# Placing the softmax and scan steps by weight, and remainders of the first branch in turns

## The chip, the core and the metric

The kernel runs on one core of a Trainium2 chip. The metric is the time of one execution in device microseconds. Three executions of the kernel before took 1069.21, 1072.25 and 1073.41 us; their median is 1072.25. Five engines work beside each other: PE (TensorE, with its weight loads shown as PEld), DVE (VectorE), ACT (ScalarE), POOL (GpSimd) and SP (SyncE, which issues transfers). Each runs its own list of instructions in the order in which they were written; what one needs from another it waits for on a semaphore.

## The reference, cut to what matters

Three network blocks follow one another on 256 tokens of width 1024 in float32. The change lies in the first one:

```python
h = rms_norm(x, norm1_g)
(dq, dk, dv, iq, ik, iw, nq, nkv, ng, sz, sxbc, sdt, mg) = split(h @ w_in)
y_a = dsa_mixer(...)                       # softmax attention over keys chosen by top-k
y_b = nsa_mixer(...)                       # compressed, selected and window attention
y_c = ssd_mixer(sz, sxbc, sdt, ...)        # short convolution, chunked scan, gate by silu(sz), norm
gates = sigmoid(mg)                        # three gates of width 1024
mix = gates[0] * (y_a @ w_br_dsa) + gates[1] * (y_b @ w_br_nsa) + gates[2] * (y_c @ w_br_ssd)
x = x + mix @ w_out
x = x + square(relu(rms_norm(x, norm2_g) @ w_ff1)) @ w_ff2
```

The second block and the final norm are left as they are by the change.

## The kernel before

Every product with a weight matrix is a job: one tile of 128 output columns by 256 tokens, accumulated in a PSUM bank of p_proj over eight blocks of 128. There are three such banks. The products are made in two parts each: a weight tile w is split into w_hi, a copy rounded to the matrix format (ACT, L1052, into ring_hi with 3 slots), and the remainder w - w_hi (L658, into ring_lo), and the activations are split in the same way (L1082 for the copy, L666 for the low part). A job is then 24 matmuls, w_hi by hi, w_hi by lo and w_lo by hi (L2056 to L2058). Weights stream into a ring of 5 slots and are used in the order of the jobs.

The planner writes one list of steps; each engine takes from it its own share, in that order. The middle of the first block is the loop over `wide`, a list of 80 jobs, numbered here 0 to 79:

- 0 to 3 gates (mg); 4 to 39 twelve times two convolution inputs (xbc) and a gate; 40 to 55 the scan's gate (sz); 56 to 63 the last eight mg; 64 to 71 br_dsa (the first branch's product); 72 to 79 br_nsa.

Behind each job stands a share of `filler`, 89 groups of other work, spread evenly by count:

- `soft`, 53 groups, one softmax step of an attention head each, as a pipeline: scores (sA, PE L1904 into p_score, released by DVE), exponentials (sE, ACT), probabilities (sR), transposes (sB, PE L1914 into the one bank p_turn, read by ACT), values (sC, PE L1932 into p_pv). Some groups carry a compressed-attention step too (pA L1883, pB, pT: four transposes L1891 into p_turn, copied out by ACT at L979) or a top-k selection on DVE (up to L1505), which a later sA waits for (`select_done`).
- `prep`, 15 groups: transposes of the convolved inputs (btr L1949; xtr L1943 into p_turn, read by DVE at L1598), states (st L1963), and others.
- `quads`, 21 groups, the scan for one of 16 head groups each: uE (ACT L1037 and L1045), the decay products on POOL (L795, L799), uB (PE L1976 into p_pv, then DVE L1619 and L1624). From step 8 on a group also holds the split of two finished tiles (ACT L1082), their squares (ACT L1118), the sum of squares over channels (PE L1988 into p_mean) and the scaled low parts (DVE L1363). The last group is the norm of the scan's output (ynorm).

So a group that holds two rows in the list stands behind one job when the count is ahead: in the kernel before, jobs 7, 14, 21, 28, 35, 42, 56, 63 and 70 carry two groups and all others one. Softmax steps end at job 46, transposes stand in jobs 47 to 57, scan steps (uE) start at job 61.

Other work stands at fixed places behind the group: the convolution of a job (xconv, DVE L1578 to L1583, which reads the bank of p_proj) behind the next job, the products with the gates (DVE L1725 for sz, L1742 for br_dsa, L1745 and L1747 for br_nsa; POOL L807 for a part of the mg gates), and the splits of the branches: the first four tiles of br_dsa's input ahead of job 63's group, the other four behind it. br_dsa's low parts alternate between DVE (even) and POOL (odd).

Who makes a remainder is set by `on_gpsimd(u)`: always POOL for some names, br_dsa among them, otherwise in turns by the number of the tile:

```python
def on_gpsimd(u):
    if unit_of[u] in ("br_dsa", "dq", "nq", "val_glu", "b_gate", "a_gate", "xr"):
        return True
    ...
    return hi_turn[u] % 2 == 0
```

The copy and the remainder of a tile that is used four jobs later stand behind each job (the steps `wsplit`).

## Time and profile before

| | |
|---|---|
| three executions | 1069.21, 1072.25, 1073.41 us |
| median | 1072.25 us |
| profiled execution | 1073.69 us |
| span of the profile | 1072.0 us |
| mean granted clock of TensorE | 0.987 |
| PE busy | 1019.9 us (95%) |
| DVE busy | 673.4 us (63%) |
| ACT busy | 618.6 us (58%) |
| POOL busy | 589.4 us (55%) |

The span is what the profiler saw from the first to the last instruction; the profiled execution's own time is 1.7 us longer. PE is busy for nearly all of it. Of the 1072 us the loop over `wide` takes the stretch from 122 to about 490 us. The granted clock is a share of full speed, 2.4 GHz; 0.5 is the lower level, 1.2 GHz.

### The profile page before, as it was taken

The numbers are of one execution on the slowest core, as the hardware profiler recorded it, in microseconds if no ns is written. First come the engines' busy times: TensorE is split into PE (matmuls) and PEld (weight loads), VectorE is DVE, ScalarE is ACT, GpSimd is POOL, SyncE is SP. The second block draws the span as 40 slices with busy tenths as digits, with TensorE's granted clock in tenths as the row PEclk, the third lists the DMA queues.
The fourth block names the chain that finished last, engine by engine and source line by source line (L and its number), as shares of the span: only waits on it lengthen the run. The fifth ranks groups of instructions, "written<-read, shape, count | busy, mean of one in ns | idle before, by whom it ended". The sixth has DMA issues, their size and how long they took to land. (4 is left out here: it accounts for less than half of the span.)

```text
span 1072.0 us, 19547 instructions
## 1 busy us (share of the span) xinstructions
PE 1019.9 (95%) x7235; PEld 922.5 (86%) x7235; DVE 673.4 (63%) x1441; ACT 618.6 (58%) x1246; POOL 589.4 (55%) x448
## 2 busy tenths in 40 slices
PE   8999999999999998889999999999899989899996
PEld 8799878888889997789989999878898977689985
DVE  7769687666564426685545554232699986478873
ACT  5455566766665448764446555344434548568853
POOL 3657344444545449844543434444768876467563
PEclk9999999999999998999999999999999999999998
DMA  8334333343333455435655555655555545634452
GB/s 311 99 119 138 119 118 99 101 120 116 100 102 116 153 177 169 153 97 178 216 180 174 180 185 187 197 176 177 158 158 158 182 152 157 216 119 146 140 171 95
DMA packets 45822, 163.76 MB, mean 153 GB/s; under 512 B 5216, under 2 KB 5280, under 8 KB 45216
## 3 DMA queue, kind: packets, MB, share of 16 engines
q1 hardware_dynamic: 43200, 158.25, 47.0%
q10 hardware_dynamic: 2528, 4.26, 1.4%
q8 instruction: 58, 0.95, 0.4%
q14 instruction: 36, 0.29, 0.1%
HBM read 161.41 MB, written 1.08 MB: 152 GB/s over the span
## 5 line engine op out<-in xcount | busy, mean ns | idle before, releaser
L658 POOL TENSOR_TENSOR ring_lo<-ring,ring_hi 128x1024 fp32r<-128x1024 f32 x176 | 425.1, 2419 | 280.3 <-ACT ring_hi L1052 279.5
L2056 PE MATMUL p_proj<-arena_r,ring_hi 128*128 128x256 f32 x1664 | 499.2, 300 | 11.0 <-POOL ring_lo L658 5.0
L2057 PE MATMUL p_proj<-arena_r,ring_hi 128*128 128x256 f32 x1664 | 473.9, 285 | 0.0
L2058 PE MATMUL p_proj<-arena_r,ring_lo 128*128 128x256 f32 x1664 | 473.8, 285 | 0.0
L1052 ACT ACTIVATE ring_hi<-ring 128x1024 fp32r<-128x1024 f32 x276 | 289.5, 1054 | 118.7 <-PE p_proj L1814 63.5
L2056 PEld LDWEIGHTS p_proj<-arena_r,ring_hi 128*128 128x128 f32 x1664 | 322.0, 194 | 27.8 <-issue 15.8
L2057 PEld LDWEIGHTS p_proj<-arena_r,ring_hi 128*128 128x128 f32 x1664 | 322.4, 194 | 7.2 <-issue 6.0
L2058 PEld LDWEIGHTS p_proj<-arena_r,ring_lo 128*128 128x128 f32 x1664 | 322.1, 194 | 0.0
L658 DVE TENSOR_TENSOR ring_lo<-ring,ring_hi 128x1024 fp32r<-128x1024 f32 x100 | 130.8, 1308 | 113.8 <-ACT ring_hi L1052 112.5
L1812 PE MATMUL p_proj<-ring_hi,arena_r 128*128 128x512 f32 x272 | 107.8, 396 | 8.0 <-POOL ring_lo L658 5.3
L1814 PE MATMUL p_proj<-ring_lo,arena_r 128*128 128x512 f32 x272 | 106.1, 390 | 0.0
L1813 PE MATMUL p_proj<-ring_hi,arena_r 128*128 128x512 f32 x272 | 106.0, 390 | 0.0
L773 POOL TENSOR_TENSOR sbuf_s<-sbuf_s,srow 128x256 f32<-128x256 f32 (+1 forms) x48 | 41.8, 871 | 83.3 <-DVE srow L1565 58.7
L1812 PEld LDWEIGHTS p_proj<-ring_hi,arena_r 128*128 128x128 f32 x272 | 51.1, 188 | 22.0 <-POOL ring_lo L658 7.8
L1082 ACT ACTIVATE arena_r<-arena 128x256 fp32r<-128x256 f32 x108 | 42.7, 409 | 39.5 <-DVE arena L1747 22.5
L1814 PEld LDWEIGHTS p_proj<-ring_lo,arena_r 128*128 128x128 f32 x272 | 51.1, 188 | 10.9
L1813 PEld LDWEIGHTS p_proj<-ring_hi,arena_r 128*128 128x128 f32 x272 | 51.1, 188 | 10.0
L666 POOL TENSOR_TENSOR arena_r<-arena,arena_r 128x256 fp32r<-128x256 f32 x59 | 45.5, 783 | 25.4 <-ACT arena_r L1082 25.4
L1214 ACT ACTIVATE th<-p_proj 128x256 f32<-128x256 f32 x44 | 16.9, 384 | 57.8 <-PE p_proj L2058 57.7
L1553 DVE CUSTOM_DVE_ANT_0 sbuf_s<-p_score,caus,nrq 128x128 f32<-128x128 f32 (+1 forms) x64 | 24.2, 415 | 41.0 <-PE p_score L1904 40.8
L1658 DVE SCALAR_TENSOR_TENSOR p_score<-arena,par,p_score 128x256 f32<-128x256 f32 x116 | 47.0, 483 | 1.2
L987 ACT ACTIVATE sbuf_s<-sbuf_s,srow 128x128 f32<-128x128 f32 (+1 forms) x96 | 42.6, 449 | 3.1 <-DVE srow L1553 3.1
(345 smaller groups left out, 1277.7 us busy)
## 6 DMA issues: line engine op xcount, KB each, us to landing
ring<-w_stream SPq DMA_DIRECT2D x286, 512.0 KB, 3.5
arena<-run_d ACTq DMA_DIRECT2D x11, 256.0 KB, 3.9
arena<-w_tok SPq DMA_DIRECT2D x1, 1632.0 KB, 12.6
arena<-w_rgi SPq DMA_DIRECT2D x1, 1536.0 KB, 6.1
wide_a<-run_d ACTq DMA_DIRECT2D x5, 256.0 KB, 4.0
arena<-x_t SPq DMA_DIRECT2D x4, 256.0 KB, 6.6
arena<-w_cmp SPq DMA_DIRECT2D x1, 1024.0 KB, 15.8
sbuf_s<-x_tok SPq DMA_DIRECT2D x1, 1024.0 KB, 5.6
```

Source lines behind the costliest of these rows:

```text
L658: return eng.tensor_tensor(ring_lo[:, u % RING, :, :].rearrange("p k n -> p (k n)"), ring[:, u % RING, :, :].rearrange("p k n -> p (k n)") ...
L666: return eng.tensor_tensor(lo(c), src(c), hi(c).bitcast(F32), ALU.subtract)
L987: ins = act.activation(p, p, ACT.Exp, bias=srow[:, i % 4, 2 + h:3 + h], scale=-1.0, accum_out=srow[:, i % 4, 4 + h:5 + h])
L1052: act.activation(ring_hi[:, hi_slot[u], :, :].rearrange("p k n -> p (k n)"), ring[:, u % RING, :, :].rearrange("p k n -> p (k n)"), ACT.Copy)\
L1082: ins = act.activation(hi(c), src(c), ACT.Copy)
L1658: ins = dve.scalar_tensor_tensor(out=A(AC + cc) if tap == CONV_K - 1 else acc, in0=ub[:, cc, tap:tap + S], scalar=col("even_cw", CONV_K * ...
L1812: pe.matmul(slot(key), hi, w_hi, start=(c == 0), stop=False)
L1813: pe.matmul(slot(key), lo, w_hi, start=False, stop=False)
L1814: mm = pe.matmul(slot(key), hi, w_lo, start=False, stop=(c == n - 1))
L2056: pe.matmul(slot(s)[:, 0:S], w_hi, hi, start=(c == 0), stop=False)
L2057: pe.matmul(slot(s)[:, 0:S], w_hi, lo, start=False, stop=False)
L2058: mm = pe.matmul(slot(s)[:, 0:S], w_lo, hi, start=False, stop=(c == n - 1))
```

## The change

The groups are no longer spread by count, but by weight. Each group has a number of units: 12 for the first ten softmax steps, 10 for the other 43, 8 for each group of `prep` and 15 for each scan group, 985 in all. A group is placed behind job n if its accumulated end does not go beyond (n + 1) / 78 of 985, that is 12.63 units per job. The order of the groups among themselves stays. And br_dsa leaves the list of `on_gpsimd`, so that its eight remainders take turns by their number: four stay on POOL and four go to DVE.

```diff
--- before.py
+++ after.py
@@ -1,3 +1,4 @@
+import itertools
 from contextlib import ExitStack
 
 import concourse.bass as bass
@@ -220,6 +221,7 @@
         quads.append(group)
     quads.append([("ynorm",)])
     filler = soft + prep + quads
+    ends = list(itertools.accumulate([12] * 10 + [10] * 43 + [8] * len(prep) + [15] * len(quads)))
     mg = jobs["mg"]
     wide = []
     wide += mg[0:4]
@@ -235,8 +237,7 @@
             out += [("split", "dsa", c) for c in range(4)]
         if job[1] == "br_dsa":
             out.append(("split", "nsa", job[2]))
-        want = (n + 1) * len(filler) // (len(wide) - 2)
-        while at < min(want, len(filler)):
+        while at < len(filler) and ends[at] * (len(wide) - 2) <= (n + 1) * ends[-1]:
             out += filler[at]
             at += 1
         if job == mg[23]:
@@ -637,7 +638,7 @@
         unit_half = {u: s[2] for u, s in enumerate(opening(steps)) if s[0] == "tm"}
 
         def on_gpsimd(u):
-            if unit_of[u] in ("br_dsa", "dq", "nq", "val_glu", "b_gate", "a_gate", "xr"):
+            if unit_of[u] in ("dq", "nq", "val_glu", "b_gate", "a_gate", "xr"):
                 return True
             if unit_of[u] == "even_yb" and unit_half[u] == 0:
                 return True
```

Lines of the changed kernel are numbered one higher than those of before from here on (L1904 is L1905, L658 is L659).

The placement that follows: two softmax steps stand in jobs 11, 15, 19, 22, 26, 30, 34, 38 and 41, and one in each other job up to 43; job 7 now has one. Transposes and states stand in jobs 44 to 51, with two groups in 44 (btr and the first xtr), 46, 47 and 49 (a state and a transpose) and 51 (the last two xtr). Scan steps start at job 55, one per job, with none in jobs 59, 65 and 71, and job 63 has one. ynorm stays in job 77.

PE, behind job 7, before. The names: sbuf_s are probabilities, sbuf_t their transposes, tok the values, kk_d keys, and arena_r the split activations.

```order
L1914 MATMUL p_turn<-ident,sbuf_s 128x128 [waits p_ready,turn_read_act]
L1914 MATMUL p_turn<-ident,sbuf_s 128x128
L1932 MATMUL p_pv<-sbuf_t,tok 64x128 [waits turn_read_act,pv_read_act]
L1932 MATMUL p_pv<-sbuf_t,tok 64x128
L1904 MATMUL p_score<-kk_d,arena 128x2x128 [waits score_read_dve]
L1914 MATMUL p_turn<-ident,sbuf_s 128x128 [waits p_ready,turn_read_act]
L1914 MATMUL p_turn<-ident,sbuf_s 128x128
L1932 MATMUL p_pv<-sbuf_t,tok 64x128 [waits turn_read_act,pv_read_act]
L1932 MATMUL p_pv<-sbuf_t,tok 64x128
L1904 MATMUL p_score<-kk_d,arena 128x512 [waits select_done,score_read_dve]
L2056 MATMUL p_proj<-arena_r_51,ring_hi 128x256 [waits w_lo_dve,proj_read_dve,proj_read_act]
```

And in the changed kernel:

```order
L1915 MATMUL p_turn<-ident,sbuf_s 128x128 [waits p_ready,turn_read_act]
L1915 MATMUL p_turn<-ident,sbuf_s 128x128
L1933 MATMUL p_pv<-sbuf_t,tok 64x128 [waits turn_read_act,pv_read_act]
L1933 MATMUL p_pv<-sbuf_t,tok 64x128
L1905 MATMUL p_score<-kk_d,arena 128x2x128 [waits score_read_dve]
L2057 MATMUL p_proj<-arena_r_51,ring_hi 128x256 [waits w_lo_dve,proj_read_dve,proj_read_act]
```

The second step, whose scores wait for the selection (`select_done`), now stands behind job 8, and job 8's first matmul directly behind the first step.

POOL, from the gate of job 62 to the second job of br_dsa, before. sqb and root are tiles that hold gates, arena_r_55 and arena_r_56 are the low parts of br_dsa's input, and sbuf_s with kk_s is a scan product.

```order
L807 TENSOR_SCALAR sqb<-sqb 128x256 [waits proj_read_act]
L799 TENSOR_TENSOR sbuf_s<-sbuf_s,kk_s 128x512 [waits l_ready]
L658 TENSOR_TENSOR ring_lo<-ring,ring_hi 128x1024 [waits w_hi_ready]
L807 TENSOR_SCALAR root<-root 128x256 [waits proj_read_act]
L666 TENSOR_TENSOR arena_r_55<-arena,arena_r_51 128x256 [waits hi_dsa] x2
L799 TENSOR_TENSOR sbuf_s<-sbuf_s,kk_s 128x512 [waits l_ready] x2
L666 TENSOR_TENSOR arena_r_56<-arena,arena_r_52 128x256 [waits hi_dsa] x2
L658 TENSOR_TENSOR ring_lo<-ring,ring_hi 128x1024 [waits w_hi_ready]
L799 TENSOR_TENSOR sbuf_s<-sbuf_s,kk_s 128x512 [waits l_ready]
L658 TENSOR_TENSOR ring_lo<-ring,ring_hi 128x1024 [waits w_hi_ready]
```

The same place in the changed kernel:

```order
L808 TENSOR_SCALAR sqb<-sqb 128x256 [waits proj_read_act]
L800 TENSOR_TENSOR sbuf_s<-sbuf_s,kk_s 128x512 [waits l_ready]
L659 TENSOR_TENSOR ring_lo<-ring,ring_hi 128x1024 [waits w_hi_ready]
L808 TENSOR_SCALAR root<-root 128x256 [waits proj_read_act]
L667 TENSOR_TENSOR arena_r_55<-arena,arena_r_51 128x256 [waits hi_dsa] x2
L800 TENSOR_TENSOR sbuf_s<-sbuf_s,kk_s 128x512 [waits l_ready]
L667 TENSOR_TENSOR arena_r_56<-arena,arena_r_52 128x256 [waits hi_dsa] x2
L796 TENSOR_TENSOR sbuf_t<-sbuf_t,arena 128x512 [waits l_ready]
L800 TENSOR_TENSOR sbuf_s<-sbuf_s,kk_s 128x512 [waits pool_chain]
L659 TENSOR_TENSOR ring_lo<-ring,ring_hi 128x1024 [waits w_hi_ready]
```

The remainder between the two gates has stayed. Between the two pairs of low parts stands one scan product in place of two. Behind the second pair stood a remainder and one scan product; now the two products of a step of the scan's second half (L796, L800) come first and a remainder behind them.

DVE, before, from the product with the gate of the first br_dsa job (job 64) on. L1742 is the product with the gate, L666 a low part of the next branch, L1619 and L1624 read the scan products.

```order
L1742 TENSOR_TENSOR arena<-p_proj,arena 128x256 [waits mg_ready,proj_filled,lo_dsa]
L666 TENSOR_TENSOR arena_r_57<-arena,arena_r_53 128x256 [waits hi_nsa,proj_read_dve]
L1619 SCALAR_TENSOR_TENSOR p_pv<-arena,par,p_pv 128x128 [waits pv_done,lo_nsa]
L1619 SCALAR_TENSOR_TENSOR p_pv<-arena,par,p_pv 128x128
L1624 TENSOR_TENSOR arena<-p_pv,arena 128x128 [waits dve_chain]
L1624 TENSOR_TENSOR arena<-p_pv,arena 128x128
L1742 TENSOR_TENSOR arena<-p_proj,arena 128x256 [waits mg_ready,proj_filled,pv_read_dve]
L666 TENSOR_TENSOR arena_r_57<-arena,arena_r_53 128x256 [waits hi_nsa,proj_read_dve]
L1619 SCALAR_TENSOR_TENSOR p_pv<-arena,par,p_pv 128x128 [waits pv_done,lo_nsa]
L1619 SCALAR_TENSOR_TENSOR p_pv<-arena,par,p_pv 128x128
L1624 TENSOR_TENSOR arena<-p_pv,arena 128x128 [waits dve_chain]
L1624 TENSOR_TENSOR arena<-p_pv,arena 128x128
```

The same engine in the changed kernel, from the remainder ahead of that product on:

```order
L659 TENSOR_TENSOR ring_lo<-ring,ring_hi 128x1024 [waits w_hi_ready,lo_dsa]
L1743 TENSOR_TENSOR arena<-p_proj,arena 128x256 [waits mg_ready,proj_filled,w_lo_dve]
L667 TENSOR_TENSOR arena_r_57<-arena,arena_r_53 128x256 [waits hi_nsa,proj_read_dve]
L1620 SCALAR_TENSOR_TENSOR p_pv<-arena,par,p_pv 128x128 [waits pv_done,lo_nsa]
L1620 SCALAR_TENSOR_TENSOR p_pv<-arena,par,p_pv 128x128
L1625 TENSOR_TENSOR arena<-p_pv,arena 128x128 [waits dve_chain]
L1625 TENSOR_TENSOR arena<-p_pv,arena 128x128
L1743 TENSOR_TENSOR arena<-p_proj,arena 128x256 [waits mg_ready,proj_filled,pv_read_dve]
L667 TENSOR_TENSOR arena_r_57<-arena,arena_r_53 128x256 [waits hi_nsa,proj_read_dve]
L659 TENSOR_TENSOR ring_lo<-ring,ring_hi 128x1024 [waits w_hi_ready,lo_nsa]
L1743 TENSOR_TENSOR arena<-p_proj,arena 128x256 [waits mg_ready,proj_filled,w_lo_dve]
L667 TENSOR_TENSOR arena_r_57<-arena,arena_r_53 128x256 [waits hi_nsa,proj_read_dve]
```

Two of the four remainders that DVE has taken over (L659) stand here, each ahead of a product with the gate, and the step of the scan between the second and the third of these products is gone, since job 65 has none.

## Rows read from the trace of the kernel before

**Rows 1.** The page's busy times: us, share of the span, instructions.

```profile
PE 1019.9 (95%) x7235; PEld 922.5 (86%) x7235; DVE 673.4 (63%) x1441; ACT 618.6 (58%) x1246; POOL 589.4 (55%) x448
```

**Rows 2.** Timeline, PE: start, us, engine, line, output and inputs, pieces, idle before.

```profile
395.24 0.28 PE L2056 MATMUL p_proj<-arena_r,ring_hi 128*128 128x256 f32 x1
...
398.12 0.28 PE L2056 MATMUL p_proj<-arena_r,ring_hi 128*128 128x256 f32 x1
```

**Rows 3.** Timeline, PE, the steps behind job 7 and the start of job 8.

```profile
150.94 0.70 PE L1904 MATMUL p_score<-kk_d,arena 128*128 128x256 f32 x2
...
153.11 1.10 PE L1904 MATMUL p_score<-kk_d,arena 128*128 128x512 f32 x2 [0.89 <-DVE arena L1505]
154.67 0.35 PE L2056 MATMUL p_proj<-arena_r,ring_hi 128*128 128x256 f32 x1 [0.46 <-issue]
```

**Rows 4.** Timeline, DVE, the convolution of job 5.

```profile
153.06 1.51 DVE L1583 SCALAR_TENSOR_TENSOR arena<-p_proj,half,arena 128x253 f32<-128x253 f32 x3
```

**Rows 5.** Timelines, PE, ACT and DVE: users of the bank p_turn.

```profile
191.99 0.60 PE L1891 MATMUL p_turn<-ident,arena 128*128 128x128 f32 x4
...
192.74 0.59 ACT L979 ACTIVATE arena<-p_turn 128x512 f32<-128x512 f32 x1
...
352.14 0.69 DVE L1598 TENSOR_TENSOR arena<-p_turn,sp 128x512 f32<-128x512 f32 x1
...
381.04 0.66 PE L1943 MATMUL p_turn<-ident,arena 128*128 128x128 f32 x4 [0.85 <-DVE arena L1598]
```

**Rows 6.** Timeline, PE, scan products behind jobs 63 and 64.

```profile
403.97 0.66 PE L1976 MATMUL p_pv<-sbuf_s,arena 128*64 128x128 f32 x8
...
409.88 1.12 PE L1976 MATMUL p_pv<-sbuf_s,arena 128*64 128x128 f32 x8 [5.26 <-DVE arena L1624]
...
416.35 0.66 PE L1976 MATMUL p_pv<-sbuf_s,arena 128*64 128x128 f32 x8
```

**Rows 7.** Timelines, POOL (three rows) and DVE, around job 64.

```profile
405.84 2.54 POOL L658 TENSOR_TENSOR ring_lo<-ring,ring_hi 128x1024 fp32r<-128x1024 f32 x1
...
408.89 1.41 POOL L666 TENSOR_TENSOR arena_r<-arena,arena_r 128x256 fp32r<-128x256 f32 x2
410.26 2.51 POOL L799 TENSOR_TENSOR sbuf_s<-sbuf_s,kk_s 128x512 f32<-128x512 f32 x2
...
405.41 3.25 DVE L666 TENSOR_TENSOR arena_r<-arena,arena_r 128x256 fp32r<-128x256 f32 x2 [10.39 <-ACT arena_r L1082]
```

**Rows 8.** Windows: stretch, us, busy PE, PEld, DVE, ACT, POOL, PEclk, DMA share, GB/s.

```profile
409.70:416.50 6.80, 6.62 (x34) 6.07 (x36) 2.84 (x7) 4.47 (x12) 6.80 (x6) 0.52 0.29 82
443.90:447.30 3.40, 3.40 (x14) 3.03 (x14) 1.95 (x6) 3.37 (x10) 0.84 (x1) 0.54 0.09 32
```

**Rows 9.** Waits of PE between 122 and 490 us: total, times, longest.

```profile
PE p_pv L1976 <- DVE arena L1624: 10.6, 5, 5.3
```

**Rows 10.** Timeline, PE, the scan's second half.

```profile
442.53 0.45 PE L1976 MATMUL p_pv<-sbuf_s,arena 128*64 128x128 f32 x4 [2.70 <-DVE arena L1624]
...
449.11 0.45 PE L1976 MATMUL p_pv<-sbuf_s,arena 128*64 128x128 f32 x4
...
454.11 0.45 PE L1976 MATMUL p_pv<-sbuf_s,arena 128*64 128x128 f32 x4
...
483.30 1.43 PE L1988 MATMUL p_mean<-th,mean_d 128*128 128x256 f32 x4 [1.65 <-ACT th L1118]
```

**Rows 11.** Timeline, DVE, two turns of the scan's second half.

```profile
469.56 0.49 DVE L1624 TENSOR_TENSOR arena<-p_pv,arena 128x128 f32<-128x128 f32 x2
...
472.66 2.65 DVE L1747 TENSOR_TENSOR arena<-arena,sqb 128x256 f32<-128x256 f32 x1
...
475.99 0.49 DVE L1624 TENSOR_TENSOR arena<-p_pv,arena 128x128 f32<-128x128 f32 x2
...
479.08 1.22 DVE L658 TENSOR_TENSOR ring_lo<-ring,ring_hi 128x1024 fp32r<-128x1024 f32 x1 [1.56 <-ACT ring_hi L1052]
...
481.91 0.49 DVE L1624 TENSOR_TENSOR arena<-p_pv,arena 128x128 f32<-128x128 f32 x2
```

## The prediction

> **What bounds the kernel now.** I read the page's busy times first: PE is busy for 1019.9 us of the span of 1072.0, so the time is PE's work plus the stretches in which PE waits or runs at half clock [rows 1]. The change adds and removes no instruction, so only those stretches can move. I number the wide jobs as the list `wide` does: jobs 0 to 39 alternate gate and convolution products, 40 to 55 are sz, 56 to 63 the last gates, 64 to 71 br_dsa and 72 to 79 br_nsa. A job with no step behind it takes 2.88 us [rows 2]. Between 122 and 490 us, where the moved steps stand, the list of waits gives PE three kinds of lost time.
>
> First, job 7 carries two softmax steps. PE waits 0.89 us for the end of a top-k selection on DVE and then 0.46 us before job 8, whose bank is free only when DVE ends the convolution of job 5 (row 153.06: ends at 154.57, PE starts at 154.67) [rows 3, 4]. That is 1.35 us. A pair of transposes at job 56 costs another 0.85 us [rows 5].
>
> Second, jobs 63 and 64. Two scan steps stand in job 63, beside the eight splits of the first branch. From the end of job 63 (403.97) to the end of job 64 (416.35) pass 12.4 us [rows 6]. The work in it is two groups of scan products at about 0.66 us and one job, 4.2 us with the gaps. So 8.2 us are lost: 5.26 idle, and job 64 at a clock of 0.52 [rows 6, 8]. Behind it stands POOL, which has a remainder of 2.54 us, two low parts (1.41 us), two scan products (2.51 us) and again two low parts in a row [rows 7].
>
> Third, the second half of the scan (steps 8 to 15, in jobs 70 to 78). Of PE's waits on L1624 (10.6 us in five) 5.3 us remain beside the 5.26, and 1.65 us on L1118 come to them [rows 9, 10]. After two of these waits the granted clock is 0.54 for 3.4 us, worth 1.6 us each [rows 8]. Together 10.2 us. In all the stretch loses 1.35 + 0.85 + 8.2 + 10.2 = 20.6 us.
>
> **The change part by part: the first ten steps (jobs 0 to 10).** They get 12 units against an even 12.6 per job, so job 7 keeps one softmax step and its second one goes to job 8. PE then reaches job 8 early, at 151.6 (the end of the product that began at 150.94). Nothing on DVE ahead of the convolution that frees the bank has moved, so job 8 starts at 154.67 as before. PE idles 3.0 us instead of 1.35: a loss of 1.7. The step itself is only done later. After idles of 2.70 and 1.65 us the clock was at 0.54 for 3.4 us [rows 8, 10]. I therefore charge another 1.6 us, bounds 0 and 1.6.
>
> **The other softmax steps (jobs 11 to 43).** Pairs now stand in jobs 11, 15, 19, 22, 26, 30, 34, 38 and 41 instead of every seventh job. A pair costs nothing beyond its work where the bank p_turn is read in time. In job 15 it is not: the transposes of the compressed probabilities (L1891) now stand directly ahead of the next step's transposes in the one bank, and ACT's copy of them ends at 193.33 where PE is done with them near 192.4. PE waits about 1.0 us where job 15 hid it before [rows 5]. For the other eight pairs I take 0; the bound is 0.5 each, 4 us, if ACT falls behind.
>
> **Transposes and states (jobs 44 to 51).** Two steps in a job share p_turn twice: btr with the first transpose in job 44, and the last two in job 51. The pair of job 56 cost 0.85 [rows 5]; I take 0.85 for job 44. In job 51 an sz gate stands on DVE ahead of the reading transposed tile (row 352.14 took 0.69 us), so the second waits about 1.4. Together 2.25 against 0.85: a loss of 1.4.
>
> **The scan's first half and the remainders in turns (jobs 55 to 64).** Steps now start at job 55, one per job, where ACT has room. Four of the eight remainders of br_dsa go to DVE, at 1.22 us (row 479.08) instead of some 2.4. Job 63 has one scan step. I count from the end of its products, T. POOL does a remainder until T+2.6, the last gate until 3.0, two low parts until 4.4, one scan product until 5.7, two low parts until 7.1 [rows 7]. DVE's even low parts stand behind the same POOL instructions: the pair at 405.41 took 3.25 us and ended just after the remainder of 405.84 [rows 7]. The last piece of job 64 starts at T+7.1 and the job ends near T+7.5; its work needs 3.5. So 4.0 us are idle, and I add 1.0 for the clock (bounds 0 and 2.4): 5.0 instead of 8.2, a gain of 3.2.
>
> **The scan's second half (jobs 66 to 77).** This is the largest term. Without waits PE takes 5.0 us for a job with such a step (449.11 to 454.11) [rows 10]. But a ring of DVE and ACT turns once per step: DVE reads the products and ends L1624; ACT then splits and squares two tiles and after that splits the next weights; DVE waits for these, makes the remainder, reads the job's bank, and only then reads the next products. From 476.48 to 482.40 one turn takes 5.9 us with the remainder on DVE; from 470.05 to 476.48 it takes 6.4 with the remainder on POOL, since L1747 took 2.65 us beside it [rows 11]. The turns in br_dsa hold a low part (L666) in place of L1747, so I keep about 6.0. Seven turns from step 8 to step 15 take 42 us. Before, the jobs 71 to 76 lay beside them; now 68 to 75, two more, because jobs 65 and 71 carry no step. PE's own work beside the seven turns is 8 × 2.88 + 7 × 1.9 = 36 us, so 6 us remain idle, in pieces of 0.2 to 1.6. One fall of the clock, half of it inside such waits, adds 0.8. That is 6.8 instead of 10.2, a gain of 3.4; bounds 2 (the turns shrink to PE's pace) and 12.
>
> The Trainium skill (page "SBUF — State Buffer", section "SBUF: two separate sides") says that GpSimd and a DVE instruction with two SBUF inputs share a port pair as an exclusive lock: the one that starts second is blocked until the other has ended. The trace agrees: L1747 began at 472.66 and ended at 475.31, while POOL's remainder ran [rows 11]. By that rule alone a remainder moved to DVE may stand behind a whole POOL instruction, which speaks against the turns; what it would give is the second rival.
>
> **The sum.** After: 4.6 + 1.0 + 2.25 + 5.0 + 6.8 = 19.6 us lost, 1.0 less than the 20.6. The profiled execution took 1073.69 (span 1072.0 and 1.7 around it); 1.0 less is 1072.7. That run lies 1.4 above the median of the three, 1072.25, so on the scale of the median I say **1071.2 us**. A measurement of this kernel can tell about 0.5% (5.4 us) from no change.
>
> **The rivals.** *The late stretch runs at PE's pace* (chance 0.29). POOL loses 4 × 2.4 = 9.6 us of work around jobs 62 to 69, and DVE's blocked instructions shrink with it. For it: POOL is what stands in the way in rows 7, and two jobs without steps break the ring. Against it: the ring has 5.9 us even where POOL is idle [rows 11]. The second half then loses 2 us instead of 6.8, and jobs 63 and 64 lose 2.7 (no fall of the clock, and DVE's low parts are early) instead of 5.0: 7.1 us off, 1064.1.
>
> *DVE becomes the bound* (chance 0.11, the slower side). Each of the four remainders put on DVE stands in the ring. If each waits for a whole POOL instruction (1.3 to 2.4 us), the four turns in br_dsa take 8 us instead of 6. It decides from about 1.3 us per remainder on, because that is the slack that jobs 65 and 71 give. Four times 1.8 us is 7.2; one more fall of the clock is 1.6: 8.8 us more, 1080.0.
>
> *The first idle does not come* (chance 0.10). If DVE reaches the bank of job 8 earlier, or PE makes the time up, the 3.3 us of the first part vanish: 1067.9. Against it stands the unchanged order on DVE.
>
> *The steps move and nothing follows* (chance 0.05): every wait is only put elsewhere, 1072.2.
>
> **How the numbers follow.** My forecast has the remaining 0.45; its own range is 1066 to 1076, from the clock charge of job 8 (1.6 less), the eight pairs (up to 4 more) and the second half (3 either way). The range reaches into the first rival and ends short of the second: 1063 to 1077.5. Faster by over 0.5% (below 1066.9): nearly all of the first rival, a third of the third and a tenth of the forecast, 0.35. Slower (above 1077.6): nearly all of the second and little of the forecast, 0.12. Within 0.5%: 0.53.
>
> **What would show it.** In the trace of the changed kernel PE should idle about 3 us ahead of job 8, with a clock near 0.5 behind it; about 1 us behind the second L1891 group; 0.9 and 1.4 us in the paired transposes near 350 to 375 us; some 4 us, in pieces, in the first job of br_dsa. The ring should turn every 6 us, with PE waits of 0.2 to 1.6 us on L1624's successor. I am wrong if PE waits under 2 us in all from job 65 to 78, if the clock stays at full ahead of job 9, or if the softmax pairs show waits on p_turn.

## The result: 1077.3 us against 1072.5

The changed kernel took 1077.34 us, the median of 20 executions (1072.15 to 1080.46); the kernel before, measured beside it, took 1072.53 us (20 executions). The ratio, which goes by all executions and not by the two medians, is 1.0032, with a 95% interval of 1.002 to 1.0044. The forecast was 1071.2 us, a little faster. The change made the kernel a little slower: by 4.8 us in the medians and 3.4 us by the ratio. That is inside the 0.5% that the prediction called no change, but the interval lies clear of no change, on the other side of it than the forecast. 1077.34 us lies outside the forecast's own range (1066 to 1076) and just inside the wide one (1063 to 1077.5).

The page of the changed kernel begins with the busy times of the engines. They answer to [rows 1]; the span is 1076.0 us, 4.0 more than before, in an execution of 1077.98 us.

```profile
PE 1024.1 (95%) x7235; PEld 925.3 (86%) x7235; DVE 683.8 (64%) x1445; ACT 619.1 (58%) x1246; POOL 583.1 (54%) x444
```

The four remainders that moved are to be seen here (DVE 4 instructions more, POOL 4 fewer). PE makes the same 7235 matmuls and is busy 4.2 us longer: a matmul at half clock counts as busy. Where PE waits, its list of waits between 122 and 490 us tells (total us, times, longest). It answers to [rows 9].

```profile
PE p_proj L2057 <- issue: 5.5, 3, 3.0
PE p_proj L2057 <- DVE arena_r L667: 3.5, 1, 3.5
PE p_pv L1977 <- DVE arena L1625: 2.0, 2, 1.3
PE p_turn L1944 <- DVE arena L1599: 1.3, 1, 1.3
PE p_proj L2057 <- POOL arena_r L667: 1.2, 2, 0.7
PE p_turn L1915 <- ACT arena L980: 0.8, 1, 0.8
PE p_turn L1944 <- ACT kk_d L1013: 0.7, 1, 0.7
PE p_turn L1915 <- ACT sbuf_t L997: 0.3, 1, 0.3
```

The 10.6 us on the scan's sums (L1624 before) have become 2.0. In their place stand jobs that wait for low parts (L667) or start late ("issue": 3.0 ahead of job 8, 2.1 ahead of job 64), and four waits on the bank p_turn. PE's timeline at the four places, as in [rows 3, 5, 6]:

```profile
150.78 0.70 PE L1905 MATMUL p_score<-kk_d,arena 128*128 128x256 f32 x2
154.51 0.35 PE L2057 MATMUL p_proj<-arena_r,ring_hi 128*128 128x256 f32 x1 [3.03 <-issue]
...
199.22 0.66 PE L1915 MATMUL p_turn<-ident,sbuf_s 128*128 128x128 f32 x4 [0.78 <-ACT arena L980]
...
413.53 0.66 PE L1977 MATMUL p_pv<-sbuf_s,arena 128*64 128x128 f32 x8
416.28 0.36 PE L2057 MATMUL p_proj<-arena_r,ring_hi 128*128 128x256 f32 x1 [2.09 <-issue]
417.35 0.39 PE L2057 MATMUL p_proj<-arena_r,ring_hi 128*128 128x256 f32 x1 [0.48 <-POOL arena_r L667]
420.41 0.58 PE L2057 MATMUL p_proj<-arena_r,ring_hi 128*128 128x256 f32 x1 [0.72 <-POOL arena_r L667]
...
463.04 0.58 PE L2057 MATMUL p_proj<-arena_r,ring_hi 128*128 128x256 f32 x1 [3.51 <-DVE arena_r L667]
```

The clock is in the windows (columns as in [rows 8]; the granted clock is the third number from the end):

```profile
155.30:158.70 3.40, 3.40 (x18) 3.40 (x17) 0.83 (x4) 1.03 (x2) 2.88 (x2) 0.50 0.02 5
418.20:428.40 10.20, 9.46 (x45) 8.31 (x44) 6.15 (x9) 5.25 (x12) 8.88 (x6) 0.50 0.29 93
463.40:469.30 5.90, 5.90 (x30) 4.99 (x30) 4.67 (x9) 3.23 (x7) 1.81 (x2) 0.50 0.27 89
```

PE was at the lower level, 1.2 GHz, for 3.4 us behind the wait ahead of job 8, for 10.2 us from inside job 64 on, and for 5.9 us behind the wait inside job 72. If half of PE's busy time there is counted as lost, that is 1.7, 4.7 and 2.95 us.

Half is a little too much. A third profile of the same kernel (E14 below) has the same wait ahead of job 8 and no half clock behind it. These are its rows of job 8's start and of the wait in job 15:

```profile
154.92 0.36 PE L2057 MATMUL p_proj<-arena_r,ring_hi 128*128 128x256 f32 x1 [3.02 <-issue]
...
198.14 0.66 PE L1915 MATMUL p_turn<-ident,sbuf_s 128*128 128x128 f32 x4 [0.78 <-ACT arena L980]
```

From the one to the other pass 43.22 us, against 44.71 us (154.51 to 199.22) in the first profile. So 3.4 us at half clock cost 1.5 us, 44% of the busy time, and by that price the three stretches cost 1.5, 4.2 and 2.6 us.

From these rows the sum of the prediction can be made again, with what was measured (the clock at half of the busy time, as the prediction counts it):

| stretch | lost before | forecast | idle, measured | clock, measured | lost, measured |
|---|---|---|---|---|---|
| jobs 7 and 8 | 1.35 | 4.6 | 3.03 | 1.7 | 4.7 |
| job 15 | 0 | 1.0 | 0.78 | 0 | 0.8 |
| the bank p_turn, jobs 41 to 56 | 0.85 | 2.25 | 0.33 + 0.69 + 1.29 | 0 | 2.3 |
| jobs 63 to 65 | 8.2 | 5.0 | 2.09 + 0.48 + 0.72 | 4.7 | 8.0 |
| the scan's second half | 10.2 | 6.8 | 0.72 + 1.32 + 3.51 | 2.95 | 8.5 |
| sum | 20.6 | 19.6 | 15.0 | 9.4 | 24.3 |

24.3 against 20.6 is 3.7 of the 4.0 us between the two spans; with 44% in place of half it is 23.3 against 20.4, and 2.9 of the 4.0 us. Every forecast of a loss is there. Of the two forecasts of a gain, that of jobs 63 to 65 is not there (8.0 against 8.2 us before) and that of the scan's second half came by half (8.5 against 10.2, where 6.8 was forecast).

### The profile page after: what moved, and what is told of

It reads as the page before. It is cut to its first block and busy times, and to the rows that moved or that the text cites. A ratio compares the mean times of both kernels' runs of the same rounds, so it can differ in the third digit from the quotient of the medians.

```text
span 1076.0 us, 19551 instructions
## 1 busy us (share of the span) xinstructions
PE 1024.1 (95%) x7235; PEld 925.3 (86%) x7235; DVE 683.8 (64%) x1445; ACT 619.1 (58%) x1246; POOL 583.1 (54%) x444
## 5 line engine op out<-in xcount | busy, mean ns | idle before, releaser
L659 POOL TENSOR_TENSOR ring_lo<-ring,ring_hi 128x1024 fp32r<-128x1024 f32 x172 | 415.4, 2419 | 286.4 <-ACT ring_hi L1053 285.6
L659 DVE TENSOR_TENSOR ring_lo<-ring,ring_hi 128x1024 fp32r<-128x1024 f32 x104 | 138.4, 1331 | 115.9 <-ACT ring_hi L1053 114.6
L667 POOL TENSOR_TENSOR arena_r<-arena,arena_r 128x256 fp32r<-128x256 f32 x59 | 46.4, 798 | 25.6 <-ACT arena_r L1083 25.5
```

What stands on the lines that cost most here:

```text
L659: return eng.tensor_tensor(ring_lo[:, u % RING, :, :].rearrange("p k n -> p (k n)"), ring[:, u % RING, :, :].rearrange("p k n -> p (k n)") ...
L667: return eng.tensor_tensor(lo(c), src(c), hi(c).bitcast(F32), ALU.subtract)
```

## The experiments

All of them were timed beside the kernel before. Its medians in the four groups below were 1073.0, 1071.9, 1072.1 and 1072.0 us, so kernels of different groups are compared by their ratios to it.

### One part of the change at a time

E1 has the new placement alone, with br_dsa's remainders all on POOL:

```diff
-            if unit_of[u] in ("dq", "nq", "val_glu", "b_gate", "a_gate", "xr"):
+            if unit_of[u] in ("br_dsa", "dq", "nq", "val_glu", "b_gate", "a_gate", "xr"):
```

> The changed kernel with br_dsa back among the remainders that POOL always makes, so only the new placement is left. The changed kernel took 1077.3 us, the one before 1072.5. Theory (the placement costs, the turns in themselves give a little): around jobs 63 to 65 POOL has two remainders of 2.4 us more, so PE's waits there, 3.3 us in the changed kernel, grow by about 2 us, and the time is 1078 to 1081. Rival (the remainders on DVE stand in the ring of the scan's second half and make job 72 late): without them the wait of 3.5 us ahead of job 72 goes and the time falls to 1073 to 1075.

E2 is the kernel before with the turns alone, the same line changed the other way.

> The kernel before with only br_dsa taken from the list, so the steps stand as before and four of eight remainders go to DVE. Theory (the placement costs, the turns give): the wait of 5.26 us behind job 63 shrinks by one remainder of POOL, about 2.4 us, and the time is 1069 to 1071. Rival (the turns cost): DVE's remainders stand in the ring of the scan's second half, PE's waits on the sums that DVE writes grow, and the time is 1074 to 1077.

E3 is the changed kernel with the first thirteen steps back where they stood:

```diff
-[12] * 10 + [10] * 43 + [8] * len(prep)
+[12] * 8 + [5, 12, 12, 12, 13] + [10] * 40 + [8] * len(prep)
```

> The changed kernel with the first thirteen softmax steps placed as in the kernel before (two behind job 7, one each behind jobs 8 to 12); the rest of the placement is that of the changed kernel. Theory: the idle time of 3.0 us ahead of job 8 becomes 1.35 us as before and the half clock behind it (about 1.5 us lost) does not come, so the time is 1073.5 to 1075. Rival (what PE wins there it loses again in the next waits, because another engine sets the pace): within 1 us of the changed kernel, 1076.5 to 1078.

E4 moves one scan step from job 72 to job 71:

```diff
-[15] * len(quads)
+[15] * 15 + [14, 16] + [15] * 4
```

> The changed kernel with one weight lowered by one unit and the next raised by one, so that the scan step of job 72 stands behind job 71 and job 72 has none. Theory (job 72 is the first to use the last low part of br_nsa's input, which DVE makes late behind POOL's remainder, and a job 71 without a step brings PE there too early): the wait of 3.5 us ahead of the last block of job 72 goes, the half clock behind it too (about 2.9 us lost), a wait of 1 to 2 us on DVE's sums comes in job 71, and the time is 1072 to 1075. Rival (the ring of DVE and ACT is simply 6 us behind PE, wherever PE meets it): the idle time moves to the next step's wait in full, and the time is 1076 to 1078.

| kernel | median us | ratio to before | interval |
|---|---|---|---|
| changed | 1077.34 | 1.0032 | 1.002 to 1.0044 |
| E1, placement alone | 1077.80 | 1.0046 | 1.0023 to 1.0068 |
| E2, turns alone | 1070.43 | 0.9979 | 0.9968 to 0.999 |
| E3, first steps as before | 1073.03 | 1.0003 | 0.999 to 1.0016 |
| E4, step in job 71 | 1078.19 | 1.0054 | 1.0035 to 1.0073 |

The wide spacing of the first ten steps costs 3 to 4 us (E3 against the changed kernel), as the theory had it, though the time is half a microsecond below its range: in E3's profile PE waits 0.89 and 0.46 us there as before, and the first stretch at half clock is gone. The rest of the placement with the turns is worth nothing (E3 against before: 1.0003).

The turns alone are worth 2 to 3 us on the old placement, and nothing on the new one (E1 against the changed kernel, whose intervals lie over each other). Neither expectation of E1 had that. Its waits show an exchange: ahead of job 64 and inside it 2.7 and 0.4 us in place of 2.1, 0.5 and 0.7; on the scan's sums 0.6 in place of 2.0; inside job 72 4.8 in place of 3.5. E2's time lies where its theory had it, but not for the reason given: the wait behind job 63 fell only from 5.3 to 4.7 us, not by 2.4. From that wait's end to the scan products behind job 64 E2 takes 5.1 us, the kernel before 6.5, of which 6.4 lie at half clock.

In E4 the rival held. Two rows of its waits, PE between 122 and 490 us:

```profile
PE p_pv L1977 <- DVE arena L1625: 5.3, 5, 1.7
...
PE p_proj L2057 <- DVE arena_r L667: 0.5, 1, 0.5
```

The wait of 3.5 us inside job 72 is nearly gone, and the waits on the scan's sums have grown from 2.0 to 5.3 us. It was not job 72 that was badly placed: the turn of DVE and ACT lags behind PE, and PE meets the lag at whatever comes first.

### The bank p_turn, the turns exchanged, and other places for the scan

For E5 the weights are replaced by a list with a job for each group, as for all that follow. It has E3's first steps, then softmax pairs behind jobs 14, 18, 21, 24, 28, 31, 35 and 38, a state and a transpose together in jobs 47 to 50 and all other transposes alone; the scan stands as in the changed kernel:

```diff
+    where = [0, 1, 2, 3, 4, 5, 6, 7, 7, 8, 9, 10, 11, 12, 13, 14, 14, 15, 16, 17, 18, 18, 19, 20, 21, 21, 22, 23,
+             24, 24, 25, 26, 27, 28, 28, 29, 30, 31, 31, 32, 33, 34, 35, 35, 36, 37, 38, 38, 39, 40, 41, 42, 43,
+             44, 45, 46, 47, 47, 48, 48, 49, 49, 50, 50, 51, 52, 53, 54,
+             54, 55, 56, 57, 58, 60, 61, 62, 63, 64, 66, 67, 68, 69, 70, 72, 73, 74, 75, 76, 77]
-        while at < len(filler) and ends[at] * (len(wide) - 2) <= (n + 1) * ends[-1]:
+        while at < len(filler) and where[at] <= n:
```

> The kernel with the first steps as before (1073.0 us), and in it the pairs moved so that no two users of the bank p_turn stand directly behind each other: softmax pairs behind jobs 7, 14, 18, 21, 24, 28, 31, 35 and 38, and the transposes one per job from 44 on, a state and a transpose together in four jobs; scan steps as in the changed kernel. Theory (the four waits on p_turn, 0.78 + 0.32 + 0.69 + 1.28 us, are a plain loss): 3.1 us less, 1069.5 to 1070.5. Rival (PE gets earlier to the scan, which POOL, DVE and ACT pace, and waits longer there): 1072 to 1073.5.

E6 is E3 with the turns of br_dsa exchanged: POOL and DVE each make the other's four remainders.

```diff
         def on_gpsimd(u):
+            if unit_of[u] == "br_dsa":
+                return hi_turn[u] % 2 > 0
```

> The kernel with the first steps as before (1073.0 us), and in it the turns of br_dsa's remainders exchanged: the four of DVE on POOL and the four of POOL on DVE. Theory (the remainder that POOL makes as job 63 ends holds up DVE's first low parts, and through them job 64): PE's wait of 2.1 us ahead of job 64 falls to about 1 us, the two waits behind it go, the fall of the clock there with them, and the time is 1069 to 1071. Rival (the other remainders come to stand in the way in their turn, POOL's next one ahead of its own low parts): 1072 to 1075.

E7 is E3 with the scan steps of jobs 63 and 64 one job later, so that job 63 has none.

> The kernel with the first steps as before (1073.0 us), and in it the scan steps of jobs 63 and 64 one job later, so that job 63 has none and job 65 has one. Theory (the step in job 63 puts a product on POOL and exponentials on ACT between the low parts that job 64 needs): the waits inside job 64 (0.5, 1.4 and 0.7 us) go, the wait ahead of it grows by the 0.7 us of PE's work that no longer covers it, and the time is 1070 to 1072. Rival (the clock falls behind the wait ahead of job 64 in any case, and that is the larger loss): 1072.5 to 1074.5.

E8 has eleven softmax pairs, so that softmax ends at job 41, and this place for the scan groups:

```diff
-54, 55, 56, 57, 58, 60, 61, 62, 63, 64, 66, 67, 68, 69, 70, 72, 73, 74, 75, 76, 77
+52, 53, 54, 55, 56, 57, 58, 59, 60, 61, 62, 65, 66, 68, 69, 71, 72, 73, 75, 76, 77
```

> The placement without collisions, with eleven softmax pairs in place of nine so that the scan starts two jobs earlier, no step in jobs 63 and 64, and the second half of the scan over jobs 65 to 75 with none in 67, 70 and 74. Theory (the second half turns once in about 6 us whatever stands beside it, so it has to be given eleven jobs): PE's waits of the second half, 5.5 us in the changed kernel, fall under 2 us, and the time is 1064 to 1068. Rival (the turn stretches with the room that it gets, because remainders and low parts of the stepless jobs come in between): 1069 to 1073.

| kernel | median us | ratio to before | interval |
|---|---|---|---|
| E5, no collisions | 1068.05 | 0.9959 | 0.9945 to 0.9972 |
| E6, turns exchanged | 1069.91 | 0.9981 | 0.9972 to 0.999 |
| E7, no step in job 63 | 1071.43 | 1.0001 | 0.9989 to 1.0012 |
| E8, scan spread | 1069.88 | 0.998 | 0.9971 to 0.999 |

E5 took off the four waits on p_turn, 3.1 us by the profile, and 0.44% or some 4.7 us in the time: more than the theory. Its executions have a mean granted clock of 0.991 against 0.989 in E3, so one or two of these microseconds may be the clock's. All of its waits between 122 and 490 us:

```profile
PE p_proj L2057 <- DVE arena_r L667: 3.5, 1, 3.5
PE p_proj L2057 <- issue: 2.9, 3, 2.1
PE p_pv L1977 <- DVE arena L1625: 2.0, 2, 1.3
PE p_score L1905 <- DVE arena L1506: 0.9, 1, 0.9
```

So in these runs a pair of steps was free where something else of PE stood between two users of p_turn, and cost the reading engine's time where not. PE did not wait longer in the scan for coming there earlier. The waits inside job 64 (2.5 us in E3) are gone from this list too, but nothing is gained there: from the scan products behind job 63 to those behind job 64 pass 9.5 us in E5 and 9.3 in E3, since in E5 the job runs at half clock instead.

E6 took off 0.22%, 2.4 us. Here DVE's remainder and then its first pair of low parts (the first fence), and POOL's gate and low parts (the second):

```profile
409.26 2.08 DVE L661 TENSOR_TENSOR ring_lo<-ring,ring_hi 128x1024 fp32r<-128x1024 f32 x1 [1.45 <-ACT ring_hi L1055]
411.37 1.38 DVE L669 TENSOR_TENSOR arena_r<-arena,arena_r 128x256 fp32r<-128x256 f32 x2
```

```profile
410.22 1.38 POOL L810 TENSOR_SCALAR root<-root 128x256 f32<-128x256 f32 x1
411.57 1.77 POOL L669 TENSOR_TENSOR arena_r<-arena,arena_r 128x256 fp32r<-128x256 f32 x2
```

In the changed kernel the pair on DVE took longer, 2.08 us, since a remainder on POOL (413.55 to 415.90) lay beside it:

```profile
413.55 2.35 POOL L659 TENSOR_TENSOR ring_lo<-ring,ring_hi 128x1024 fp32r<-128x1024 f32 x1
```

```profile
414.63 2.08 DVE L667 TENSOR_TENSOR arena_r<-arena,arena_r 128x256 fp32r<-128x256 f32 x2 [2.12 <-ACT arena_r L1083]
```

The wait ahead of job 64 fell only from 2.1 to 1.8 us, not to 1 as the theory said: now DVE's own remainder, 2.08 us long beside POOL's instructions, ended just as the pair began (409.26 + 2.08 = 411.34). The waits inside job 64 (2.5 us in E3) went, as the theory said. The fall of the clock there did not go.

E7 and E8 are misses. In E7, whose 1071.43 us lies in the theory's range only because the kernel before was faster in that group too, the waits inside job 64 went, the one ahead of it grew from 2.1 to 2.7 us, and a new one of 2.0 us came ahead of job 80, where a remainder on DVE ends late; the time is that of E3. In E8 the time is the rival's: the waits of the second half fell from 5.5 only to 3.0 us, not under 2 as the theory said, and ahead of job 64 and inside it PE waits 2.5 and 3.0 us; the 2.0 us ahead of job 80 are there too.

### Together

E9 is E5 with the exchanged turns of E6; E10 is E8 with them and with one step each in jobs 63 and 64; E11 is the kernel before with nothing but the exchanged turns; E12 is E9 with the scan steps of jobs 69 and 70 in jobs 70 and 71.

> The placement without collisions (1068.1 us) with the turns of br_dsa's remainders exchanged, which took 3.1 us off the kernel with the first steps as before (1073.0 to 1069.9). Theory (the two act at different places, the bank p_turn before 375 us and POOL's remainder at job 63): the gains add up, 1064 to 1066. Rival (part of both was the same fall of the clock behind job 63, which goes once): 1066.5 to 1068.5.

> As the spread scan (1069.9 us), with exchanged turns and with one step each in jobs 63 and 64 again (none in 59, 62, 67, 70 and 74). Theory (the wait of 3.0 us inside job 64 of the spread scan came from POOL's remainder ahead of its own low parts, and what remains of waits in the second half is under 3 us): 1064 to 1066.5. Rival (the second half, however spread, hands its lag to the weights behind it: the wait of 2.0 us ahead of job 80 stays, and the waits at job 64 stay too): 1067 to 1070.

> The kernel before with br_dsa's remainders in exchanged turns and nothing else; in the turns of the change the same placement took 1070.4 us against 1072.5 to 1073.0. Theory (at job 63 POOL's remainder holds up DVE's low parts here too, and exchanging the turns takes it away): the wait of 4.7 us behind job 63 falls by 1 to 2 us, 1067.5 to 1069.5. Rival (with two steps in job 63 it is the second step's sum that ends the wait, not the low parts): 1070 to 1071.5.

> The placement without collisions and with exchanged turns (1066.7 us), with the scan steps of jobs 69 and 70 one job later, so that job 69 has no step instead of job 71. Theory (the wait of 3.5 us ahead of the last block of job 72 is for a low part that stands on DVE behind one turn of the scan too many): that low part comes one turn of about 6 us earlier against PE, the wait goes, some 1 to 2 us of it come back at the sums of the steps, and the time is 1063 to 1066. Rival (PE is ahead of the turns of the scan as a whole and waits as long, only elsewhere): 1066 to 1068.

| kernel | median us | ratio to before | interval |
|---|---|---|---|
| E9, no collisions, exchanged | 1066.65 | 0.9951 | 0.9935 to 0.9967 |
| E10, spread, exchanged | 1070.36 | 0.9989 | 0.9978 to 0.9999 |
| E11, before, exchanged | 1069.66 | 0.9979 | 0.9968 to 0.999 |
| E12, as E9, job 69 free | 1066.10 | 0.9939 | 0.9922 to 0.9957 |

E9 and E12 are faster than the kernel before and the changed one, by 0.5 and 0.6% of the former; they cannot be told from each other. The gains of E5 and E6 do not add up (E9 against E5: 0.08%, inside the intervals), so the rival of E9 held in the time. That it is the clock, as it said, is not shown but likely: E9's executions have a mean granted clock of 0.989 against 0.991 in E5 (0.990 in E6), and span times one less the clock is some 2 us more in E9 than in E5, in six and eight executions. In E10 the rival held, in a time a little above its range: PE waits 4.4 us ahead of job 64 and inside it, 3.5 us in the second half and 2.0 us ahead of job 80. On the old placement the exchanged turns of E11 give no more than the turns of E2 did (1069.66 us, between the two ranges); there PE waits 5.0 us for the second step's sum, as the rival said. E12's waits are the test of what the wait inside job 72 is:

```profile
PE p_pv L1979 <- DVE arena L1627: 3.3, 4, 1.1
...
PE p_proj L2059 <- DVE ring_lo L661: 2.0, 1, 2.0
...
PE p_proj L2059 <- DVE arena_r L669: 0.7, 2, 0.5
```

The wait for the low part went from 3.5 to 0.5 us. But 3.3 us on the scan's sums (0.8 in E9) and 2.0 on a remainder came for it. E4, E8 and E12 say the same: the lag of the scan's second half is paid once, wherever PE meets it, and no place for the steps that was tried made it smaller in sum without a wait elsewhere.

### The same kernel again

The clock was still open. The changed kernel ran twice more for its profile alone.

> The changed kernel once more, for a second profile. Its executions of the comparison lie between 1072 and 1080 us, with a mean granted clock of 0.991 in the shortest and 0.981 in the longest. Theory (the waits are the same in each execution, and what differs is how long the clock stays at half behind the waits of jobs 8, 63 and 64 and 72): the idle times are within 0.3 us of the first profile each, and the half-clock stretch behind job 63 is another than 10.3 us whenever the time is another than 1078. Rival (the waits themselves differ): idle times that differ by over 1 us at one of the places.

> The changed kernel a third time, with the same expectations as for the second profile: by the theory the same idle times and half-clock stretches whose sum moves with the time (about 1 us of time for each 2 us at half clock); by the rival different idle times.

E13 took 1078.00 us, E14 1072.92 us. E13 has the waits of the first profile to 0.3 us, and its three half-clock stretches (0.50 in each of the same three windows). E14's waits, PE between 122 and 490 us:

```profile
PE p_proj L2057 <- issue: 5.5, 3, 3.0
PE p_proj L2057 <- DVE arena_r L667: 3.5, 1, 3.5
...
PE p_proj L2057 <- POOL arena_r L667: 1.1, 2, 0.6
...
```

They are those of the first profile to 0.1 us. E14's windows, behind job 8, behind the wait ahead of job 64, and behind the wait inside job 72:

```profile
155.30:158.70 3.40, 3.40 (x30) 3.06 (x30) 1.22 (x6) 2.00 (x4) 2.48 (x2) 1.00 0.02 5
416.60:420.00 3.40, 3.26 (x17) 2.97 (x17) 3.30 (x5) 3.40 (x10) 3.40 (x4) 0.58 0.33 81
420.00:424.00 4.00, 3.35 (x30) 2.84 (x29) 2.39 (x7) 2.38 (x4) 3.75 (x4) 1.00 0.44 135
460.00:463.40 3.40, 3.40 (x22) 2.71 (x19) 3.19 (x9) 2.08 (x5) 0.74 (x1) 0.56 0.47 154
463.40:466.80 3.40, 3.40 (x32) 3.27 (x31) 1.33 (x2) 2.78 (x7) 3.32 (x3) 0.94 0.00 0
```

Behind the same 3.0 us of waiting ahead of job 8 the clock stayed at 1.00. Behind the same 2.1 us ahead of job 64 it was at half for one stretch of 3.4 us and back at 1.00 from 420 us on, where the first profile has 10.2 us. Behind job 72 it was low for 3.4 us in place of at least 5.9. The theory held and the rival fell: the waits are the same in each of the three profiles, the clock is not. Only its price was off: E14 is 5.1 us faster with some 13 us less at half clock, 1 us for 2.6 and not for 2.

That fits the spread of the executions. Of the 20 of the changed kernel seven took 1072.15 to 1073.81 us, all with a mean granted clock of 0.991; the other thirteen took 1075.86 to 1080.46 us at 0.981 to 0.988.

## Why the prediction was wrong

**The first ten steps: right.** PE waited 3.03 us ahead of job 8 (forecast 3.0), and the clock fell behind it in two of three profiles (1.5 us; forecast 1.6, bounds 0 and 1.6). In the third it stayed at full ahead of job 9, which the prediction had named as a sign of being wrong, with the same idle time ahead of it. E3 puts the price of the place at 3 to 4 us in the time.

**The other pairs: right, where they were costed.** Job 15 waited 0.78 (forecast 1.0), jobs 44 and 51 0.69 and 1.29 (0.85 and 1.4). (The kernel before has two groups in jobs 49 and 77 as well; the state and transpose in job 49 cost no wait there.) Of the eight softmax pairs costed at nothing seven waited for nothing and the one in job 41 0.33 us. E5, without these waits, is faster by about as much or more, so they were a plain loss.

**Jobs 63 to 65: the idle time right, the clock and a pair of low parts mis-sized.** 3.3 us idle were measured, 4.0 forecast. The clock was charged with 1.0 us, bounds 0 and 2.4. Of the 10.2 us at half clock PE was busy for 9.46 in the first profile (the second is like it); in the third it was busy for 3.3 us at a mean of 0.58. What that makes of the time is seen from the scan products behind jobs 63, 64 and 66. They begin at 413.53 us (shown above) and then, in the first profile:

```profile
423.02 1.12 PE L1977 MATMUL p_pv<-sbuf_s,arena 128*64 128x128 f32 x8
...
431.88 0.66 PE L1977 MATMUL p_pv<-sbuf_s,arena 128*64 128x128 f32 x8
```

And in the third:

```profile
412.46 0.66 PE L1977 MATMUL p_pv<-sbuf_s,arena 128*64 128x128 f32 x8
...
421.00 0.39 PE L2057 MATMUL p_proj<-arena_r,ring_hi 128*128 128x256 f32 x1 [0.65 <-POOL arena_r L667]
421.56 0.66 PE L1977 MATMUL p_pv<-sbuf_s,arena 128*64 128x128 f32 x8
...
428.10 0.66 PE L1977 MATMUL p_pv<-sbuf_s,arena 128*64 128x128 f32 x8
```

Three jobs, two of them with such a step, take 10.2 us where PE neither waits nor is slow (3.65 us from step to step behind jobs 62 and 63, 2.88 for a job without one). 18.35 us passed in the first profile and 15.64 in the third, so 8.2 and 5.5 us were lost; forecast were 5.0. The waits are the same to 0.1 us, so the 2.7 us between the two are the clock's, and 2.3 of them lie behind job 64 (8.86 us against 6.54). In job 64 itself (9.49 against 9.10) the low clock cost little: its last block needs POOL's second pair of low parts, and in the third profile PE waits 0.65 us for it. The forecast gain of 3.2 us was there by 2.7 with the shorter stretch and not at all with the longer.

That pair of low parts is a smaller step that failed. The prediction counted it at 1.4 us, done 7.1 us after T, the end of job 63's scan products. It took 2.57 us and was done 7.8 us after T (413.53 + 0.66 = 414.19; 419.45 + 2.57 = 422.02), in all three profiles beside one of the remainders that the change had moved to DVE. In E1, where DVE makes none of them, it took 1.60 us, and job 64 took 8.8 us in place of 9.5. The changed kernel's POOL and DVE, then E1's POOL:

```profile
419.45 2.57 POOL L667 TENSOR_TENSOR arena_r<-arena,arena_r 128x256 fp32r<-128x256 f32 x2
...
419.81 1.63 DVE L659 TENSOR_TENSOR ring_lo<-ring,ring_hi 128x1024 fp32r<-128x1024 f32 x1
```

```profile
419.45 1.60 POOL L667 TENSOR_TENSOR arena_r<-arena,arena_r 128x256 fp32r<-128x256 f32 x2
```

So a remainder moved from POOL to DVE can hold up POOL as well, by 1.0 us here.

**The second half of the scan: the clock again.** 5.55 us idle against 6 forecast. (The forecast's own rows give less: with 5.0 us for a job with a step and 2.88 for one without, a step is 2.1 us and not 1.9, PE's work 38 us and not 36, and the idle time 4 us. That 6 came out so near is in part luck.) The idle time came in pieces of 0.7 to 3.5 us rather than of 0.2 to 1.6: seven turns of DVE and ACT at about 6 us are in the trace, but PE met most of the lag in one place, the last block of job 72, since job 71 has no step at which it would have met it earlier. There DVE's last low part of br_nsa's input ended late for a reason that the prediction had put among the rivals:

```profile
460.35 2.35 POOL L659 TENSOR_TENSOR ring_lo<-ring,ring_hi 128x1024 fp32r<-128x1024 f32 x1 [0.53 <-ACT ring_hi L1053]
```

```profile
456.16 0.42 DVE L667 TENSOR_TENSOR arena_r<-arena,arena_r 128x256 fp32r<-128x256 f32 x1
...
460.68 2.30 DVE L667 TENSOR_TENSOR arena_r<-arena,arena_r 128x256 fp32r<-128x256 f32 x1
```

A low part of the same size that began at 456.16 us took 0.42 us, this one 2.30, where it began behind a remainder of POOL and ended 0.28 us after it (460.35 + 2.35 = 462.70; 460.68 + 2.30 = 462.98). By the Trainium skill (page "SBUF — State Buffer", section "SBUF: two separate sides") the one of GpSimd and a DVE instruction with two SBUF inputs that starts second is blocked until the other has ended; the trace agrees. The clock was charged with 0.8 us and cost 2.6 to 2.95 us in the first profile and 1.5 in the third.

So of the five terms of the sum three held to 0.2 us, and the idle times of the other two came out 0.5 to 0.7 us below the forecast. What failed in both is above all one step: the price of the clock. The forecast's gain hung on it alone. By its own terms the idle time was to grow, from 14.4 us (1.35 + 0.85 + 5.26 + 5.3 + 1.65) to 16.25 (3.0 + 1.0 + 2.25 + 4.0 + 6), and the time lost to the clock to fall from 6.2 us to 1.6 + 1.0 + 0.8 = 3.4. The first two profiles show 8.3 us for it (9.4 at half of the busy time), and the third about 3. The prediction had taken the 3.4 us at half clock of [rows 8] as what one wait costs and made the charge smaller where it expected shorter waits. But behind the waits ahead of job 64 and inside job 72 the clock fell in every profile of the changed kernel, and how long it then stayed low was not to be read from the wait.

By the third profile the changed kernel took 1072.9 us, near the 1072.7 of the forecast's sum against the profiled execution. That is in part luck: no clock was lost behind job 8, where 1.6 us were charged, and about as much was lost where nothing was charged (the pair of low parts, and what is said below of PE's own pieces). The median lies elsewhere because thirteen of twenty executions, by their mean clock, have longer stretches at half clock. That the kernel before has fewer of these (29 executions of it, beside E1 to E4, had a mean granted clock of 0.986 to 0.992) was not in its single profile.

**The rivals.** The late stretch did not run at PE's pace. DVE did not become the bound through its four remainders: E1, without them, took the same time. The first idle came. That nothing follows from moving the steps is answered by E3 and E5, whose times differ.

**What stays open.** Span times one less the granted clock, in the mean over all executions, is 14.0 us for the changed kernel and 12.8 for the one before (the 29 beside E1 to E4). So 1.2 of the 3.5 us between the mean times (1076.1 and 1072.7) are clock by that measure, where the forecast had the clock's share fall by 2.8. The measure is rough: it puts the first and the third profile, with the same waits, 6.5 us apart, and their spans differ by 5.1. But at the same clock the changed kernel is slower too: its seven executions at 0.991 took 1072.9 us in the mean, and ten executions of the kernel before, of the 94 beside the experiments, with 0.991 to 0.994 took 1070.2. So some 2.3 to 2.7 us are not the clock's. The first profile shows 0.6 us more idle time than the one of before. About 1 us more is in PE's own pieces, by an estimate from the traces: from the start of one matmul to that of the next, without the waits and with half clock priced at 44%, PE's instructions between 87 and about 495 us come to 382.5 us in all three profiles of the changed kernel and to 381.4 to 381.6 in those of the kernel before, E2 and E11 (381.8 in E5 and E9). Why the pieces are longer, and what makes up the remaining microsecond, was not found.

## What to carry to other kernels

Cost a moved step by the bank or engine that reads it next, as here for p_turn: these terms held to 0.2 us, and taking the collisions away gave the only large gain. When a wait of TensorE behind which the clock fell is moved or shortened but not removed, don't count the time at half clock behind it as gone: give it the whole range that the executions show, and look at the granted clock of several executions before pricing it from one profile. A group of instructions that lags behind is paid for once; moving the place where the fast engine meets it (E4, E8, E12) moved the wait and did not shorten the time clear of the noise. Work handed from POOL to DVE is not free for POOL: look at what POOL does beside it.

## What the runs showed of the hardware

How long the clock stays at half was not the same for the same wait. From job 64 on it was 10.2 us in two profiles of the changed kernel and 3.4 in the third, for the same waits of 2.1 us ahead of that job and 1.1 to 1.4 inside it. Nor was it longer where PE waited more: E3, with 2.1 us ahead of job 64 and 2.5 inside it, was low for most of 3.6 us, and E5, with 2.1 us and none inside, for 9.8:

```profile
418.30:421.90 3.60, 3.52 (x19) 2.97 (x20) 1.95 (x6) 1.49 (x3) 3.34 (x4) 0.55 0.73 196
```

```profile
408.90:418.70 9.80, 9.55 (x42) 8.12 (x43) 7.76 (x14) 6.94 (x16) 9.56 (x8) 0.50 0.35 113
```

The first is E3's window, the second E5's. PE was busy in nearly all of both, so it did not fall silent again in the longer one. What makes the difference, the runs don't tell. E5 is nevertheless 0.44% faster than E3: three more microseconds lost to the clock in its profile were outweighed, and over its executions the mean clock is the higher (0.991 against 0.989).

A low clock is not always lost time. In job 64 it lay beside waits for POOL that PE would otherwise have met: the job took 9.5 us in the first profile and in E5 and 9.1 to 9.3 in the third profile and E3, where PE was less at half clock and waited at its last block.
